# The order and the row capacities of the expert blocks in a one-core encoder layer: full and light experts in turns

## What is computed

```
def hierarchical_moe(x, ...):        # 32 experts in 4 groups of 8, top-2 inside the best group
    grp   = top_k(group_logits, 1)
    top   = top_k(expert_logits of grp, 2);  gate = softmax(top) * group_prob
    for each expert e, for the rows xb of x that chose e:      # 2 * 1536 = 3072 rows in all
        h = silu(xb @ w1[e]) * (xb @ w3[e])                    # 1024 -> 512, twice
        y = h @ w2[e]                                          # 512 -> 1024
        out[row] += gate * y
```

## Time and profile before

| | us |
|---|---|
| median of 3 timed runs | 1596.06 |
| lowest and highest | 1595.56 to 1600.31 |
| the profiled execution | 1602.02 |
| its span, first to last instruction | 1600.4 |
| start of step 2, of step 4, of step 16, of step 31 (chain) | 948.7, 992.9, 1235.5, 1530.3 |

### The profile page before, as it was taken

One profiled execution on the slowest core, in us unless ns is written; L12 is line 12 of the kernel. 1 busy time (PEld: TensorE's weight loads), 2 busy tenths in 40 slices (PEclk: granted clock), 3 DMA queues, 4 the chain that ended last, 5 costly groups with the idle time before them and its releaser, 6 DMA issues.

```text
span 1600.4 us, 32656 instructions
## 1 busy us (share of the span) xinstructions
PE 1491.9 (93%) x13884; PEld 948.3 (59%) x13884; DVE 524.3 (33%) x1085; ACT 394.0 (25%) x577; POOL 185.2 (12%) x244
## 2 busy tenths in 40 slices
PE   7999999999999997999893899999999999999990
PEld 3444445555555554545451778777777777777750
DVE  3860035535536545454458201111111111111114
ACT  4120044454446434222440100000000000000004
POOL 2011000110010010011101111111111111111110
PEclk9999999999999998999995899999999999999995
DMA  6132132233123314435582949999999999999968
GB/s 231 40 105 86 66 138 73 73 106 110 63 98 102 118 68 142 160 138 204 201 288 101 361 148 320 360 359 355 357 356 353 357 367 361 367 364 363 365 199 328
DMA packets 75254, 350.07 MB, mean 219 GB/s; under 512 B 9704, under 2 KB 22504, under 8 KB 62752
## 3 DMA queue, kind: packets, MB, share of 16 engines
q1 hardware_dynamic: 56624, 288.31, 48.7%
q0 software_dynamic: 17968, 58.97, 12.4%
q10 hardware_dynamic: 576, 1.59, 0.3%
HBM read 285.69 MB, written 63.14 MB: 218 GB/s over the span
## 4 chain that ended last, share of the span: by engine, by line
PE 52%; DVE 3%; DMA 2%; ACT 2%; issue 2%; DVEq 0%; SPq 0%; POOLq 0%; ACTq 0%
PE bank L1947 24%; PE bank L1965 13%; PE bank L1762 7%; PE bank L1835 2%; PE bank L1920 2%; DMA wup<-w 1%; PE bank L1853 1%; ACT junk L1077 1%; PE bank L1847 1%; PE bank L1705 0%; PE bank L1980 0%; DVE wide L1359 0%; DMA x_dram<-mid,sidx 0%; DVE early L1505 0%; PE bank L1714 0%
## 5 line engine op out<-in xcount | busy, mean ns | idle before, releaser
L1613 PE MATMUL bank<-wide,mid 128*128 128x512 f32 x960 | 422.0, 594 | 1.1 <-issue 1.1
L1947 PEld LDWEIGHTS bank<-xgT,wup 128*64 128x64 f32 (+1 forms) x7680 | 396.2, 141 | 29.6 <-issue 23.7
L1947 PE MATMUL bank<-xgT,wup 128*64 128x104 f32 (+3 forms) x7680 | 403.1, 258 | 5.9 <-issue 3.4
L1613 PEld LDWEIGHTS bank<-wide,mid 128*128 128x128 f32 x960 | 179.4, 190 | 213.5 <-issue 212.8
L1965 PE MATMUL bank<-wide,hidT 128*128 128x512 f32 x512 | 225.6, 593 | 1.6 <-DVE mid L1546 1.6
L1965 PEld LDWEIGHTS bank<-wide,hidT 128*128 128x128 f32 x512 | 94.8, 190 | 109.5 <-issue 107.1
L1537 DVE TENSOR_TENSOR hidT<-sil,bank 128x512 f32<-128x512 f32 x30 | 20.6, 688 | 348.8 <-PE bank L1947 298.2
L1762 PE MATMUL bank<-early,mid 128*128 128x512 f32 x288 | 129.2, 603 | 2.5 <-issue 2.5
L804 POOL DMA_INDIRECT x_dram<-mid,sidx x32 | 50.2, 1568 | 535.1 <-DVE gidx L1523 484.3
L1060 ACT ACTIVATE sil<-bank 128x512 f32<-128x512 f32 x30 | 17.9, 597 | 381.5 <-PE bank L1947 381.5
L1546 DVE TENSOR_SCALAR mid<-bank,gate_of 128x512 f32<-128x512 f32 x64 | 48.0, 751 | 192.8 <-PE bank L1965 192.8
(11 more groups left out here) (250 smaller groups left out, 1254.9 us busy)
## 6 DMA issues: line engine op xcount, KB each, us to landing
wup<-w SPq DMA_DIRECT2D x64, 2048.0 KB, 16.1
wide<-w SPq DMA_DIRECT2D x32, 2048.0 KB, 10.1
u_dram<-ustage POOLq DMA_DIRECT2D x60, 256.0 KB, 2.3
rin<-u_dram SPq DMA_DIRECT2D x60, 256.0 KB, 4.4
mid<-w_in SPq DMA_DIRECT2D x23, 512.0 KB, 3.6
wide<-x_t SPq DMA_DIRECT2D x12, 512.0 KB, 11.5
mix_dram<-mixst POOLq DMA_DIRECT2D x24, 256.0 KB, 2.7
mid<-x_all SPq DMA_DIRECT2D x12, 512.0 KB, 5.5
```

The lines of the kernel that those rows point to most:

```text
L1613: last = pe.matmul(PROJ[u % 3][:, :], wsec[:, slot, k, :], nT[:, k, g * GT:(g + 1) * GT], start=(k == 0), stop=(k == KT - 1))
L1947: last = pe.matmul(target[c0:c0 + wide_tile, at:at + rows], weights[:, s, k, f * P + c0:f * P + c0 + wide_tile], xgT[:, k, 0:rows], start= ...
```

## The change

Three things. First, a fourth step of capacities: 128 from rank 0, 112 from rank 4, 104 from rank 14 (before: 16), 96 from rank 22. Second, a map from rank to block: ranks 0 and 1 keep blocks 0 and 1; behind them rank r goes to block 2r - 2, or, where that is beyond 65 - 2r, to block 65 - 2r. So even blocks 2, 4, ..., 30 hold ranks 2, 3, ..., 16, and odd blocks 3, 5, ..., 31 hold ranks 31, 30, ..., 17. Third, the loop's segments take a pair of capacities, for the even and for the odd block, and there are five of them instead of three: blocks 4 and 5 (128, 96), 6 to 21 (112, 96), 22 to 25 (112, 104), 26 to 29 (104, 104), 30 and 31 (104, 104).

```diff
-CAPACITY = ((0, 128), (4, 112), (16, 104))
+CAPACITY = ((0, 128), (4, 112), (14, 104), (22, 96))
 def capacity(b):
-    return [rows for first, rows in CAPACITY if first <= b][-1]
+    r = b if b < BIG_BLOCKS else (NE - b // 2 if b % 2 else b // 2 + 1)
+    return [rows for first, rows in CAPACITY if first <= r][-1]
...
-            ends = [b for b, rows in CAPACITY if b > first] + [MAIN_BLOCKS - 2, MAIN_BLOCKS]
+            ends = [b for b in range(first + 2, MAIN_BLOCKS - 2, 2)
+                    if (capacity(b), capacity(b + 1)) != (capacity(b - 2), capacity(b - 1))]
+            ends += [MAIN_BLOCKS - 2, MAIN_BLOCKS]
             for start, end in zip([first] + ends[:-1], ends):
+                rows = [capacity(start), capacity(start + 1)]
                 with eng.Fori(0, (end - start) // 2) as i:
                     for j in range(2):
-                        body(2 * i + (start + j), (start + j) % 2, capacity(start),
-                             P if j and end == MAIN_BLOCKS else capacity(start))
+                        body(2 * i + (start + j), (start + j) % 2, rows[j],
+                             P if j and end == MAIN_BLOCKS else rows[1 - j])
...
-            link(dve.tensor_scalar(main_slot[:, :], rank[:, :], float(P), None, ALU.mult))
-            for i, (first, rows) in enumerate(CAPACITY[1:]):
-                link(dve.tensor_scalar(cap_step[:, i, :], rank[:, :], ...))
-            link(dve.scalar_tensor_tensor(out=cap[:, :], in0=cap_step[:, 0, :], ...))
+            link(dve.tensor_scalar(turn[:, 0, :], rank[:, :], 2.0, -2.0, ALU.mult, ALU.add))
+            link(dve.tensor_scalar(turn[:, 1, :], rank[:, :], -2.0, float(2 * NE + 1), ALU.mult, ALU.add))
+            link(dve.tensor_scalar(turn[:, 2, :], rank[:, :], float(BIG_BLOCKS - 1), None, ALU.min))
+            link(dve.tensor_tensor(turn[:, 0, :], turn[:, 0, :], turn[:, 1, :], ALU.min))
+            link(dve.tensor_tensor(main_block[:, :], turn[:, 0, :], turn[:, 2, :], ALU.max))
+            link(dve.tensor_scalar(main_slot[:, :], main_block[:, :], float(P), None, ALU.mult))
+            link(dve.tensor_scalar(cap_step[:, :], rank[:, :], ...))
+            for first, _ in steps[1:]:
+                link(dve.scalar_tensor_tensor(out=cap_step[:, :], in0=rank[:, :], ...))
+            link(dve.tensor_scalar(cap[:, :], cap_step[:, :], ...))
...
-            link(dve.scalar_tensor_tensor(out=bcmp[:, 0:NE], in0=rank[:, :], scalar=row_id[:, 0:1],
+            link(dve.scalar_tensor_tensor(out=bcmp[:, 0:NE], in0=main_block[:, :], scalar=row_id[:, 0:1],
```

More of the change, by code:

```diff
@@ L53 @@
 FT = FE // P
-CAPACITY = ((0, 128), (4, 112), (16, 104))
+CAPACITY = ((0, 128), (4, 112), (14, 104), (22, 96))
+FEWER = 8
 MAIN_BLOCKS = NE
 SIX = 6
-MAX_OVER = -(-(2 * T // (CAPACITY[-1][1] + 1)) // SIX) * SIX
+LEAST, LESS = CAPACITY[-1][1] + 1, CAPACITY[-2][1] + 1
+LATE = min(NE, 2 * T // LEAST) - CAPACITY[-1][0]
+MAX_OVER = -(-(LATE + (2 * T - LATE * LEAST) // LESS) // SIX) * SIX
 BIG_BLOCKS, MORE = 2, 32
@@ L253, in trunk_program @@
         rank = sb(blockwise, "rank", [P, NE])
+        turn = sb(blockwise, "turn", [P, 3, NE])
+        main_block = sb(blockwise, "main_block", [P, NE])
         cap = sb(blockwise, "cap", [P, NE])
-        cap_step = sb(blockwise, "cap_step", [P, len(CAPACITY) - 1, NE])
+        cap_step = sb(blockwise, "cap_step", [P, NE])
         main_slot = sb(blockwise, "main_slot", [P, NE])
@@ L1440, in _ @@
             link(dve.tensor_reduce(rank[:, :], above[:, :, :], axis=AX.X, op=ALU.add))
-            link(dve.tensor_scalar(main_slot[:, :], rank[:, :], float(P), None, ALU.mult))
-            for i, (first, rows) in enumerate(CAPACITY[1:]):
[L1444 to L1447, removed]
+            link(dve.tensor_scalar(turn[:, 0, :], rank[:, :], 2.0, -2.0, ALU.mult, ALU.add))
[4 more added lines that the diff above has]
+            link(dve.tensor_scalar(main_slot[:, :], main_block[:, :], float(P), None, ALU.mult))
+            steps = [(first, (CAPACITY[i][1] - rows) // FEWER) for i, (first, rows) in enumerate(CAPACITY[1:])]
+            assert all(n == 1 for _, n in steps[1:])
+            link(dve.tensor_scalar(cap_step[:, :], rank[:, :], float(steps[0][0]), float(steps[0][1]),
+                                   ALU.is_ge, ALU.mult))
+            for first, _ in steps[1:]:
+                link(dve.scalar_tensor_tensor(out=cap_step[:, :], in0=rank[:, :], scalar=float(first),
+                                              in1=cap_step[:, :], op0=ALU.is_ge, op1=ALU.add))
+            link(dve.tensor_scalar(cap[:, :], cap_step[:, :], -float(FEWER), float(CAPACITY[0][1]),
+                                   ALU.mult, ALU.add))
             link(dve.tensor_tensor(bcount[:, :], count, cap[:, :], ALU.subtract))
```

## The result

| | before | changed |
|---|---|---|
| median, 9 runs each | 1600.28 us | 1589.16 us |
| lowest and highest | 1595.56 to 1600.83 | 1587.79 to 1592.93 |
| the profiled execution | 1602.02 | 1589.7 |
| its span | 1600.4 | 1588.1 |

The ratio is 0.9943, 95% interval 0.9934 to 0.9951: 9.1 us faster (11.1 by the medians), where 6.0 had been forecast (0.38%). The median of the kernel before came out at 1600.28 with nine runs, 4 us above that of the three runs that stood ahead of the prediction.

A forecast was written before the change was run, and what follows sets the result against it. PE was taken to bound the 112-row stretch, DMA the 104-row one and the changed blocks; blocks -7.3 us plus routing +1.3 gave -6.0, from 1596.06 to 1590.0 us, range 1583 to 1598.

The forecast's parts named there:

- the first rival: Blocks: PE stays the bound, DMA in timed runs keeps up with 19.3 us a block; gain 9.7 us, 1586.4; chance 0.20.
- PE's part: Steps 2 to 30: 96-row up projection 10.70 us, pair 38.60; if PE alone counted, 16.1 us sooner, 11.0 of it less work.
- The weight loads: 96-row up projections: loads expected not to hold them up; if they did with PE as bound, 0.86 us lost on ten steps, 1595.0.
- The DMA's part: Blocks 4 to 31: DMA ends last, 39.56 us a pair against PE's 38.60; step 31 at 1523.0, blocks gain 7.3 us.
- the pace of 19.78 us a block: DMA's time per block, read from w1 landings 14 blocks apart in the 104-row stretch, applied to 27 blocks.
- The rival of 355 GB/s: DMA keeps the 112-row stretch's pace, 19.95 us per 104-row block: 1594.7, no change; chance 0.22 shared with other no-change reasons.
- The light steps: Rival: light steps come too soon, w1 takes up to 19.2 us to land, pair 40.5 us; 1604.0, slower; chance 0.10.
- The routing's 1.3 us: Between rank and bcount: six more linked DVE instructions, uncovered on the path, cost 1.3 us (0 to 2).
- At nothing: Changes of loop between blocks 5/6, 21/22, 25/26: code fetch hidden by matmuls, priced at nothing, at most 1.3 us each.

The follow-up runs named there:

- half of w2: Only half of w2 loaded for each block: in the kernel before 1595.0 us (ratio to before 0.9972), in the changed kernel 1588.7 us (0.9928).
- turns of 16: Changed kernel with capacities 128, 112 from rank 4, 96 from rank 15: 1594.8 us; also without the code of the loop over further blocks: 1579.9 us.
- the order alone: Changed kernel with the capacities of the kernel before (112 from rank 4, 104 from rank 16): 1596.6 us, ratio to before 0.9979.
- the capacities alone: Changed kernel with block number = rank as before, new capacities kept: 1602.9 us, ratio 1.0026; without the code of the loop over further blocks 1591.1 us.

## Why the prediction was right, and where it was not

**The number and the sign held** (1590.0 forecast, 1589.16 measured), by -9.1 us against a baseline that itself rose, not by -6.0. That the number came so close is luck: the baseline of three runs was 4.2 us low and the gain was forecast 3 to 5 us too small, and the two cancel. The measured ratio on the old baseline of 1596.06 would be 1587.0, nearer to the first rival's 1586.4 (chance 0.20) than to the forecast.

**PE's part held to a tenth.** 96 rows: 10.71 us, foreseen 10.70. The pair 38.63 against 38.60; step 3 ends at 989.51 (989.4). The weight loads didn't hold up the light step. By an estimate from the Trainium skill's rule for loads ("TensorE: Matmul & The Clock Gate", LDWEIGHTS: columns / 1.2 ns, so 53 ns for 64 columns) they would have; the row contradicts it a second time, with 10.71 us over 128 pairs of products, 84 ns.

**The DMA's part failed at one term: the pace of 19.78 us a block.** I had read it from blocks of 104 rows and carried it over to pairs of 112 and 96, because the bytes are the same. The pairs ran at 19.32 a block, and that was PE's pace; w1 landed after 15.7 to 17.3 us, with no growth over fifteen steps. So the forecast's "the DMA is what ends last" was wrong for blocks 6 to 21, and the first rival (PE stays the bound) described them. But its reason, that timed runs have a faster DMA, was wrong: the timed runs of the kernel before do wait for it (half of w2: 4.5 us less by the ratio, 5.7 by the medians). The pace isn't set by bytes alone: with 112 rows moved instead of 104 the same blocks went faster, 291.7 us instead of 294.8. From block 22 on, where every second and then every block has 104 rows, the waits came back. Step 31 started at 1517.8 instead of 1523.0 (the forecast without the routing's 1.3 us, which didn't come out in the end); those 5.2 us are this term: the blocks gained 12.5 where 7.3 were forecast. The rival of 355 GB/s is out: 369 over 309 us. With it goes, for this one core, the limit of 358 GB/s on the Trainium skill's page "DMA: Bandwidth & Descriptors" (Specifications).

**The light steps were not too soon.** w1's time to landing was 15.7 to 17.3 us in the pairs; its 19.2 was the sign of a full queue and not a property of the load, as the argument against that rival had it.

**The routing's 1.3 us came and left no trace in the end.** The ten instructions stand there:

```profile
859.58 0.18 DVE L1450 TENSOR_SCALAR turn<-rank 128x32 f32<-128x32 f32 x1
...
861.78 0.21 DVE L1467 TENSOR_TENSOR bcount<-upto,cap 128x32 f32<-128x32 f32 x1
```

2.20 us where it was 0.87. Yet step 2 starts within 0.05 us of its old place in the profile. Of the 1.3 us, 0.7 was gone because the routing began that much earlier in this execution (855.84 against 856.52), so that the first up projection of 64 products started 0.60 us later (893.60 against 893.00); and it took 10.34 us instead of 10.98: the granted clock returned to 2.4 GHz a little earlier in the execution (0.88 against 0.70 in the window from 896 to 898 us, 1.00 in both from 898 on), while the work came later. That is one execution each. Over the profiles of five kernels with each routing, step 2 starts at 946.81 to 948.68 with the new one and at 946.23 to 948.73 with the old, at the mean 0.1 us apart; but the two kernels with turns of 16, whose routing has nine of the ten instructions, start it at 949.47 and 950.60. The scatter is larger than the 1.3 us, so that such instructions are free isn't shown.

**"At nothing" was too low for the segments.** I had priced a change of loop at no more than 1.3 us and at nothing by preference. The half of w2 shows 0.4 to 1.5 us at four places, the order alone 2.7 in one step; in the changed kernel's own profile it is 0.1 to 0.2 at two. It was outweighed by the pace. That code behind the last block could cost 8 to 9 us of standing and more in all (11.8 and 14.9 by the medians) was in no rival, and it is as much as the whole change is worth, or more.

## What to carry to other kernels

Read the pace of a saturated DMA only for the shape of transfers that you will have: here 112 rows went faster than 104. Letting heavy and light steps take turns is worth the waits of the stretch that asks too much, here about 3 us, while smaller light blocks bring the whole of their products only if they don't all stand in one DMA-bound stretch (8.1 us of 10.1 in the capacities alone). And where an edit that changes only the amount or place of code moves the time by 10 us, look at the idle time "issue" in front of the first instruction behind a long stretch of code that isn't run; compare variants with that code taken out, or the stop decides the comparison.

## What the runs showed of the hardware that was not expected

- Gathers and scatters of 104 rows beside 6.3 MB of weights a block: 366 GB/s with waits; of 112 rows at the same 104-column products: 372 GB/s with fewer.
- PE's stop in front of the last down projection has two sizes, 1.2 to 1.6 us and 8.0 to 9.4 us, in kernels of one design; in the three with the long one two packets of code arrive within it, and behind it the product ran at 1.2 GHz for part of its length (8.93 to 10.11 us instead of 7.13).
- A stop of PE in the middle of an up projection or of the transposes with no wait named, 0.4 to 1.2 us, on the first pass through new code, with a packet of code on q8 1 to 2 us ahead of it (six of seven).
